# Attention units stepped between parts of the big products in a two-layer transformer half

## The reference, cut to what matters

```
for layer in range(2):                                  # first block
    h = rmsnorm(x, norm_mix[layer])
    z = h @ w_in[layer]                                 # 1024 -> 2964
    o_a = nsa_mixer(...)      # slc, win, cmp branches: 3 softmax attentions, 4 heads of 64
    o_b = diff_mixer(...)     # two softmaxes a head, one subtracted; head rmsnorm
    o_c = mlstm_mixer(...)    # conv, gates, decay-weighted attention; head rmsnorm, times sigmoid
    o_d = dilated_mixer(...)  # attention over keys at strides 1, 4, 16
    x = x + concatenate([o_a, o_b, o_c, o_d]) @ w_out[layer]
    h = rmsnorm(x, norm_ffn[layer])
    x = x + (silu(h @ w_gate[layer]) * (h @ w_up[layer])) @ w_down[layer]
x = rmsnorm(x, norm_final)
for layer in range(2):                                  # second block
    x = conformer or gated convolution, layer norm
    x = mixture of 32 experts over all tokens, layer norm
```

## Time and profile before

| | us |
|---|---|
| median of 3 runs (2234.66 to 2235.66) | 2235.55 |
| the profiled execution | 2232.91 |
| its span, first to last instruction | 2231.1 |
| TensorE busy (share of span) | 2112.0 (95%) |
| VectorE busy | 671.6 (30%) |
| ScalarE busy | 327.8 (15%) |
| GpSimd busy | 83.3 (4%) |
| mean granted TensorE clock | 0.940 |

### The profile page before, as it was taken

One profiled execution on the slowest core, in us unless ns is written; L12 is line 12 of the kernel. 1 busy time (PEld: TensorE's weight loads), 2 busy tenths in 40 slices (PEclk: granted clock), 3 DMA queues, 4 the chain that ended last, 5 costly groups with the idle time before them and its releaser, 6 DMA issues.

```text
span 2231.1 us, 23016 instructions
## 1 busy us (share of the span) xinstructions
PE 2112.0 (95%) x9082; PEld 1217.3 (55%) x9082; DVE 671.6 (30%) x1263; ACT 327.8 (15%) x777; POOL 83.3 (4%) x124
## 2 busy tenths in 40 slices
PE   8988999999988999999899999999898899999996
PEld 4566667665565767776544444443585444444442
DVE  2254333323262333256411111111423311111113
ACT  2243000011241000022210111110101111111010
POOL 3101000001002000020000000000000000000000
PEclk9866999999858999999899999999998899999999
DMA  9311777563104777644389999999824499999995
GB/s 277 87 57 10 264 256 264 196 243 108 57 1 164 263 259 269 228 145 148 150 330 421 427 427 427 428 429 426 341 113 189 196 426 427 425 427 428 427 428 225
DMA packets 154934, 603.12 MB, mean 270 GB/s; under 512 B 16688, under 2 KB 72880, under 8 KB 127440
## 3 DMA queue, kind: packets, MB, share of 16 engines
q1 hardware_dynamic: 149728, 591.43, 67.8%
q0 software_dynamic: 4752, 10.20, 1.8%
q10 hardware_dynamic: 352, 0.06, 0.0%
HBM read 597.64 MB, written 1.10 MB: 268 GB/s over the span
## 4 chain that ended last, share of the span: by engine, by line
PE 90%; DVE 4%; DMA 2%; issue 1%; ACT 1%; DVEq 1%; SPq 0%; ACTq 0%
PE ps L1657 29%; PE ps L685 14%; PE ps L497 7%; PE ps L691 7%; PE ps L1643 6%; PE ps L1627 5%; PE ps L1545 4%; PE ps L664 3%; PE ps L1510 3%; PE ps L1558 3%; DMA ring<-in_e_w_up 2%; PE ps L629 2%; PE ps L607 1%; PE ps L563 1%; PE ps L562 1%
## 5 line engine op out<-in xcount | busy, mean ns | idle before, releaser
L685 PE MATMUL ps<-hT,ring 128*128 128x256 f32 x1408 | 313.3, 384 | 1.7 <-DVE hT L260 1.7
L685 PEld LDWEIGHTS ps<-hT,ring 128*128 128x128 f32 x1408 | 276.9, 198 | 33.7 <-issue 4.0
L1657 PE MATMUL ps<-ring,qkT 128*64 128x512 f32 x1024 | 226.8, 595 | 2.9 <-ACT qkT L1829 2.9
L1657 PE MATMUL ps<-ring,hT 128*64 128x512 f32 x1024 | 226.1, 594 | 3.4 <-DMA ring<-in_e_w_gate 1.9
L1657 PE MATMUL ps<-ring,late 128*64 128x512 f32 x1024 | 226.1, 594 | 2.9 <-ACT late L1816 2.9
L497 PE MATMUL ps<-ring,hT 128*128 128x512 f32 (+1 forms) x384 | 166.1, 591 | 3.4 <-DMA ring<-in_w_in 1.9
L1657 PEld LDWEIGHTS ps<-ring,hT 128*64 128x64 f32 x1024 | 71.9, 137 | 153.4 <-issue 146.5
L1657 PEld LDWEIGHTS ps<-ring,late 128*64 128x64 f32 x1024 | 72.8, 137 | 150.7 <-issue 150.7
L691 PE MATMUL ps<-ring,late 128*128 128x512 f32 x352 | 154.7, 592 | 0.0
L1657 PEld LDWEIGHTS ps<-ring,qkT 128*64 128x64 f32 x1024 | 72.4, 137 | 136.3 <-issue 134.5
L1643 PE MATMUL ps<-qkT,O 128*128 128x256 f32 x512 | 138.7, 417 | 3.0 <-DVEq L2062 3.0
(11 more groups left out here) (367 smaller groups left out, 1818.6 us busy)
## 6 DMA issues: line engine op xcount, KB each, us to landing
ring<-in_e_w_gate SPq DMA_DIRECT2D x64, 2048.0 KB, 15.1
ring<-in_e_w_down SPq DMA_DIRECT2D x64, 2048.0 KB, 13.5
ring<-in_e_w_up SPq DMA_DIRECT2D x64, 2048.0 KB, 16.2
ring<-in_ada_w SPq DMA_DIRECT2D x24, 2048.0 KB, 9.6
ring<-in_w_gate SPq DMA_DIRECT2D x22, 1024.0 KB, 8.2
ring<-in_w_up SPq DMA_DIRECT2D x22, 1024.0 KB, 10.1
ring<-in_w_down SPq DMA_DIRECT2D x22, 1024.0 KB, 12.6
ring<-in_w_in SPq DMA_DIRECT2D x8, 2048.0 KB, 14.2
```

The source lines that it names most:

```text
L685: last = mm(m.ps[:, c, at:at + SEQ], w[:, j, c, :], m.hT[:, j, :], start=(j == 0), stop=(j == KC - 1))
L1657: last = mm(m.ps[x * T:(x + 1) * T, out + n, :], operand[:, j, at + x * T:at + (x + 1) * T], w[x][:, j, n * 512:(n + 1) * 512], start=(j = ...
```

## The change

z products can be issued in halves of four contraction steps, and w_out products in parts of two steps for one tile. The attention units now run in the middle of these. Only the chunks NSA, U, MIX and DIFF are computed ahead of the units, with scores of units 0 and 1 between them. In each unit's round TensorE issues transposed(u), one piece of dense work (`ahead_of_values`), values(u), scores(u+2), and for some u a batch (`behind_scores`). The dense piece is half a tile of z VALUES or DIL for units 0 to 7 and a part of w_out for units 9 to 13; unit 8 has four transposes.

PSUM is laid out anew: one pair of banks for scores (0, 1), one pair for transposes and values together (2, 3), z in 4 and 5, batches in 6 and 7, w_out sums in 4 to 7. Slots are too: U lies in slot 5, MIX in 1, VALUES in 3, DIL in 4; w_out is loaded to slots 5 and 2, attention buffers lie in slot 0 and half of 1. The compression batch moves behind scores(4), the order of units changes (cmp 0 ahead of dil), and the head norms are one step for mlstm and one for diff.

The core of the diff; of moved lines only the new place is shown:

```diff
-CHUNKS = ((0, ((0, 512),)), (1, ((1420, 1932),)), (5, ((512, 652), (1932, 2196))), (2, ((652, 1164),)), (3, ((2196, 2708),)),
-          (4, ((1164, 1420), (2708, 2964))))
+CHUNKS = ((0, ((0, 512),)), (5, ((1420, 1932),)), (1, ((512, 652), (1932, 2196))), (2, ((652, 1164),)),
+          (3, ((1164, 1420), (2708, 2964))), (4, ((2196, 2708),)))
-UNITS = [("slc", 0, 0), ("mlstm", 0, 0), ("slc", 1, 0), ("mlstm", 1, 0), ("diff", 0, 0), ("diff", 1, 0), ("diff", 0, 1),
-         ("diff", 1, 1), ("win", 0, 0), ("dil", 1, 0), ("dil", 0, 0), ("win", 1, 0), ("cmp", 0, 0), ("cmp", 1, 0)]
+UNITS = [("slc", 0, 0), ("slc", 1, 0), ("mlstm", 0, 0), ("mlstm", 1, 0), ("diff", 0, 0), ("diff", 1, 0), ("diff", 0, 1),
+         ("diff", 1, 1), ("win", 0, 0), ("win", 1, 0), ("cmp", 0, 0), ("dil", 0, 0), ("dil", 1, 0), ("cmp", 1, 0)]
-OUT_PAIRS = ((2, 3), (4, 5), (6, 7), (0, 1))
+OUT_BANK = (6, 3, 0, 1, 0)
+OUT_PARTS = ((4, 0, 2), (2, 0, 2), (0, 0, 1), (6, 0, 2), (0, 1, 2))
...
 def first_sync
+            if k < 2:
+                sp.wait_ge(s["pv"], nth(L, "pv", N_UNITS))
+            elif k == 2:
+                sp.wait_ge(s["y_ps"], nth(L, "y_ps", 4))
...
             elif u == 1:
-                sp.wait_ge(s["pv"], nth(L, "pv", len(UNITS)))
+                sp.wait_ge(s["y_ps"], nth(L, "y_ps", 4))
...
 def first_tensor
+        def z_part(n, i, part):
+            c = CHUNKS[n][0]
+            if part == 0:
+                if i == 0:
+                    pe.wait_ge(m.ring_full[c], chunk_full(L, n))
+                if n > 0:
+                    pe.wait_ge(s["z_act"] if i == 0 else s["z_dve"], nth(L, "z_act", n))
+            w = m.slot[c][:, 0:KC * chunk_width(n)].rearrange("p (j n) -> p j n", j=KC)
+            for j in range(KC // 2 * part, KC // 2 * (part + 1)):
+                last = mm(m.ps[:, 4 + i, 0:chunk_width(n)], m.hT[:, j, i * P:(i + 1) * P], w[:, j, :], start=(j == 0), stop=(j == KC - 1))
...
+        def out_part(i, first):
+            for c in range(2):
+                w = m.w_out[c].rearrange("p (j n) -> p j n", j=KC)
+                for j in (first, first + 1):
+                    last = mm(m.ps[:, 4 + 2 * i + c, :], m.hT[:, j, i * P:(i + 1) * P], w[:, j, :], start=(j == 4), stop=(j == (7, 1)[i]))
...
+        def ahead_of_values(u):
+            if u < 4:
+                z_part(C_VALUES, u // 2, u % 2)
+            elif u < 8:
+                z_part(C_DIL, u // 2 - 2, u % 2)
+            elif u == 8:
+                pe.wait_ge(s["o_final"], nth(L, "o_final", 1))
+                out_transposes(0)
+            elif u == 9:
...
+                out_ready(0)
+                out_part(0, 4)
+            elif u == 10:
+                pe.wait_ge(s["prep_ev"], nth(L, "prep_ev", N_PREP))
+                out_part(1, 4)
+            elif u == 11:
+                out_ready(1)
+                out_part(0, 2)
+            elif u == 12:
+                out_part(1, 2)
+            else:
+                out_ready(2)
+                out_part(0, 0)
+                out_transposes(3)
+        def behind_scores(u):
+            if u == 1:
+                diff_batch()
+            elif u == 2:
+                cmp_batch()
+            elif u == 8:
+                dil_batch()
+            elif u == 10:
+                pe.wait_ge(s["o_final"], nth(L, "o_final", 2))
+                out_transposes(1)
+            elif u == 12:
+                pe.wait_ge(s["masked"], nth(L, "masked", N_UNITS))
+                out_transposes(2)
+        for u in range(N_UNITS):
+            transposed(u)
+            ahead_of_values(u)
+            values(u)
+            if u + 2 < N_UNITS:
+                scores(u + 2)
+            behind_scores(u)
+        out_ready(3)
+        out_part(0, 6)
+        out_part(1, 6)
+        pe.wait_ge(s["o_done"], nth(L, "o_done", N_UNITS))
+        out_transposes(4)
+        out_ready(4)
+        out_part(1, 0)
...
 def first_scalar
+        for u in range(N_UNITS):
+            transposed_out(u)
+            if u == 1:
+                z_out(C_VALUES)
+            if u == 5:
+                z_out(C_DIL)
+                head_root(0)
+            if u == 8:
+                out_taken(0)
+            if u == 9:
+                head_root(1)
+            if u + 2 < N_UNITS:
+                exponentials(u + 2)
...
+            if u == 8:
+                qk(B_DIL, T_DQ, 4)
+            if u == 10:
+                out_taken(1)
+            if u == 12:
+                out_taken(2)
...
 def first_vector
+        for u in range(N_UNITS):
+            if u + 1 < N_UNITS:
+                probabilities(u + 1)
+            if u == 3:
                 z_out(C_VALUES)
+            if u == 7:
+                z_out(C_DIL)
+            unit_out(u)
+            if u + 2 < N_UNITS:
+                masked(u + 2)
+            if u == 4:
+                sub_squared(0)
+            if u == 5:
+                sub_scaled(0)
+            if u == 6:
+                dve.wait_ge(s["z_act"], nth(L, "z_act", C_DIL + 1))
+                rotate_dil(0)
+            if u == 7:
+                dve.drain()
+                rotate_dil(1).then_inc(s["rope"], 1)
+            if u == 8:
+                sub_squared(1)
+            if u == 9:
+                sub_scaled(1)
```

More of the change, by code:

```diff
@@ new lines, in cmp_batch @@
+        def cmp_batch():
+            pe.wait_ge(m.ring_full[1], (L + 1) * 64)
+            pe.sem_inc(m.seen, 1)
+            pe.wait_ge(s["blocks"], nth(L, "blocks", 1))
+            dst = batch(B_CMP)
+            cw = m.cmp_w
+            for l in range(CMP_LEN):
+                mm(dst[0:HD, 0:N_CMP], cw[0:HD, l, :], m.blocks[0:HD, l, :], start=(l == 0), stop=(l == CMP_LEN - 1))
+                last = mm(dst[0:N_CMP, 512:512 + HD], m.blocks[HD:P, l, :], cw[HD:P, l, :], start=(l == 0), stop=(l == CMP_LEN - 1))
+            last.then_inc(s["prep_ps"], 1)
@@ L742, in qk, with exponentials @@
         def qk(b, at, count):
[L743 removed]
+            src = banks(m, 6, 2)[:, 0:count * SEQ].rearrange("p (s t) -> p s t", t=SEQ)
             evac(b, m.qkT[:, at:at + count, :], src).then_inc(s["prep_ev"], 1)
+        def exponentials(u):
+            kind, t, g = UNITS[u]
+            nk = keys_of(kind, t)
+            act.wait_ge(s["masked"], nth(L, "masked", u + 1))
+            if u >= 2:
+                act.wait_ge(s["pt_ps"], nth(L, "pt_ps", u - 1))
+            scale = 1.0 if kind == "mlstm" else 32 ** -0.5 if kind == "diff" else HD ** -0.5
+            for v in range(4):
+                h = VIEW[v]
+                bias = m.nM[:, t, h:h + 1] if kind == "mlstm" else m.nmx[u % 2][:, v:v + 1]
+                a(m.pr[:, u % 2, v, 0:nk], m.sm[:, u % 2, v, 0:nk], ACT.Exp, bias=bias, scale=scale, accum_out=m.zs[u % 2][:, h:h + 1])
+            act.drain().then_inc(s["exps"], 1)
@@ L897, in first_vector, with masked @@
         last.then_inc(s["blocks"], 1)
-        z_out(C_DIFF)
+        z_out(C_MIX)
+        dve.wait_ge(s["z_act"], nth(L, "z_act", C_MIX + 1))
+        dve.drain()
+        for i in range(TILES):
+            rotate(v, dve, m, m.rz_x, m.tmp_dve, i, [(z_heads(m, i, Z_KW, 1, HD), 0, 1, HD)])
+        v.tensor_copy(m.rz_x[:, :, HD:2 * HD], m.rz_x[:, :, 0:HD]).then_inc(s["rope"], 1)
+        def masked(u):
+            kind, t, g = UNITS[u]
+            nk = keys_of(kind, t)
+            b = u % 2
+            dve.wait_ge(s["scores"], nth(L, "scores", u + 1))
+            if u >= 2:
+                dve.wait_ge(s["exps"], nth(L, "exps", u - 1))
+            mask = {"cmp": m.cmp_mask, "dil": m.dil_mask}.get(kind, m.causal)[:, t, 0:nk]
+            sm = m.sm[:, b, :, 0:nk]
+            src = m.rb[:, :, 0:nk] if kind == "mlstm" else scores_of(m, u)
+            if kind == "mlstm":
+                dve.drain()
+            last = tt(sm, src, bcast(mask.unsqueeze(1), [P, 4, nk]), ALU.add)
+            if kind != "mlstm":
+                dve.drain()
+                v.reduce_max(m.mx[b], sm, axis=AX)
+                dve.drain()
+                last = ts(m.nmx[b], m.mx[b], -(32 ** -0.5 if kind == "diff" else HD ** -0.5), None, ALU.mult)
+            last.then_inc(s["masked"], 1)
+        masked(0)
         g = m.grow
-        gates = banks(m, prep_bank(B_WIN), 2)[0:NH, 512:1024]
+        gates = banks(m, 6, 2)[0:NH, 512:1024]
         dve.wait_ge(s["prep_ps"], nth(L, "prep_ps", B_WIN + 1))
@@ L1181, in ring_counts @@
 def ring_counts():
-    loads = [DEPTH * per for per in (2, 2, 1, 1, 2, 4)]
-    frees = [6 if c in (0, 1, 5) else 2 for c in range(N_SLOTS)]
+    loads = [DEPTH * per for per in (1, 4, 2, 2, 1, 2)]
+    frees = [DEPTH] * N_SLOTS
     out = {}
```

601 lines of the change are left out of this document (267 added, 334 removed).

## The result

The changed kernel takes 2196.38 us in the median of four runs (2194.55 to 2197.45), the kernel before beside it 2235.11: a ratio of 0.9828, interval 0.9813 to 0.9842. The forecast was 2198, faster. The profiled execution took 2197.37 us against 2232.91 before, 35.5 less, at a mean granted clock of 0.959 against 0.940.

The account below looks back on a forecast made before the run. TensorE's half-clock small matmuls, short waits and clock recovery bound the attention stages. Per layer 225.3 - 204.8 - 1.6 = 18.9 us saved, 38 for both: profiled 2232.9 to 2195, median 2198 (2190 to 2212, chance 0.50).

Parts of the forecast that it names:

- Part 1: Order up to the first unit: z 52.9, batches 7.2, two scores 1.7, 1.5 allowed for ScalarE; T(0) starts at 63.3 us.
- the batch: Compression batch behind scores(4): moved, not changed, 18.0 us as before, mostly at half clock.
- hole 1: Unit 8: only four transposes to put in, TensorE waits about 5 us, clock lost; round 10 takes 12.3 instead of 7.7.
- hole 2: Unit 11: out_part(0, 2) waits for ScalarE's out_taken(1), clock down again; round takes 13.5 us instead of 8.35.
- The bound: Attention stages: small matmuls at half clock, short waits on VectorE and clock recovery cost time; the stretch averaged 225.3 us.
- The pieces: Full-clock prices: scores 1.05 us (256 keys), values 0.95 (eight instructions), transposes 0.45 (four); exponentials 2.45, copy 1.02, 0.6 or 0.4.
- The ring: Units 4 to 13: scores, mask, exponentials, copy and values set each round, dense half product inside; first round 7.4 us.
- (a): Rival: clock lost only in the compression batch, units 8 and 11 keep it; 26.9 us a layer, 2182; chance 0.20.
- (b): Rival: clock lost in nearly every unit, seven more times, only dense parts paying 1.8 each; 2223 us; chance 0.15.
- (c): Slower rival: clock lost likewise, small matmuls at half too, 3.4 us a unit; 2246; chance 0.10 for both slower rivals together.
- (d): Slower rival: ScalarE's order puts dense parts after the waits everywhere; 2268 us; chance 0.10 for both slower rivals together.
- Part 4: Outside the units: head norms counted in the rounds, tail plus 1.6 us on 4.96, SyncE's queue nothing, at worst 2 a layer.

Follow-up runs that it names:

- kernel without stepping: Changed kernel with z computed ahead of unit 0 and five w_out parts behind the last unit; new layout kept: 2283.22 us, ratio 1.0215.
- five blocks: Changed kernel with the compression batch cut into five parts, behind scores(4) to scores(8): 2180.81 us, ratio 0.9754.
- woven kernel: Against the kernel with the compression batch in five parts: its steps put two by two between the products of A(3) to A(6): 2175.32 us.
- thinned: Changed kernel with six of eight steps of VALUES and DIL tiles and half of five w_out parts left out: 2185.38 us, ratio 0.9775.
- changed tail: Changed kernel with tile 0's norm and its transposes ahead of the last w_out part for tile 1: 2201.3 us, ratio 0.9853.
- early copy: Changed kernel with ScalarE copying transposed(u+1) ahead of exponentials(u+2) in every round: 2187.64 us, ratio 0.9789.

## Why the prediction was right, step by step

| step | forecast | layer 0 | layer 1 |
|---|---|---|---|
| Part 1: first z product to T(0) | 63.3 | 64.1 | 62.0 |
| to scores(5), with the batch | 111.5 | 113.2 | 112.8 |
| of this the batch | 18.0 | 19.7 | 19.0 |
| rounds from scores(5) | 7.4, 6.35, 7.3, 6.4, 8.0 | 7.30, 6.09, 7.24, 7.17, 8.76 | 7.30, 6.10, 7.23, 6.38, 8.76 |
| round of unit 10, behind hole 1 | 12.3 | 9.74 | 9.85 |
| next | 6.0 | 6.22 | 6.21 |
| round behind hole 2 | 13.5 | 14.07 | 14.13 |
| scores(13) to the end | 24.2 | 24.3 | 24.3 |
| z to last w_out product | 204.8 (203.0 + 1.8) | 204.2 | 203.1 |
| tail | 4.96 + 1.6 | 6.6 | 6.6 |

**The bound.** TensorE loses its clock in small work: right. (The first dip lies in slices 2 to 4 of the clock row, not 3 to 5 as the prediction reads it; nothing in the sum rests on that.) Of the three things that it says cost time, the short waits gave nothing on balance: what the dense parts fill, the new ring opens again, and TensorE's idle time in the stage is as long as before. The kernel without stepping is the same finding made large, with the clock at 0.50 in every window from 150 to 185 us.

**The pieces.** Estimates of S, V and T at full clock came from rows at half; from start to start they are now 1.06 (256 keys), 1.04 (eight instructions) and 0.50 (four), where 1.05, 0.95 and 0.45 were forecast. The copy and the exponentials were as said.

**The ring** (Part 3) held to 0.3 us in the first three rounds. The fourth was 0.8 longer in layer 0, as the clock fell for a part of it (granted 0.66 in 145 to 150 us, the dense part at 147.97 took 4.19), and in layer 1, where the clock held, it took the forecast time. So the 1.8 that the prediction added for one more loss is 0.8 in one layer and nothing in the other. The fifth was 0.8 longer in both, and this belongs to the hole: values(8) stands behind it in the same round and takes 1.90 from start to start, where eight instructions take 1.0 at full clock; the prediction charged the half clock only from the next round on.

**The batch** was mis-sized by 1.7 in layer 0 and 1.0 in layer 1: in layer 0 it ran at full clock for its first seven rows only, then at 0.32 for two instructions where 0.21 is the full rate. Before, it held the clock longer: 1.00 from 70 to 75 us, 0.50 only then.

**The two holes** were put at the right places with the right size (5 forecast, 4.70 and 4.64 measured) and the clock fell behind both. The term that was off is the price of the first: 12.3 forecast, 9.74 measured. The prediction let the dense part A pay for the return of the clock, 5.7; it took 3.65. The clock had come back ahead of it, behind 6.3 us of values, scores and transposes without a pause (0.50 in 160 to 165, 0.88 in 165 to 170). That small work had already been counted at half clock, and the dense part was then charged for the return a second time. It does not hold for every kind of small work: the batch ran for 18 us without a pause at 0.50. At unit 11 nothing small stood between the hole and the dense part, and there it took 6.5.

**The errors cancel,** in layer 0: +0.8 to T(0), +0.9 up to scores(5), +1.1 in five rounds, -2.6, +0.2, +0.6, +0.1. Together +1.1 on the 203.0, where 1.8 had been allowed. So the total is closer than its terms, which are off by up to 2.6, and that is luck. So is a part of the last step: the stages gave 40.2 us where 38 was forecast, and 4.7 of it came back outside them.

**The rules weighed.** In the batch the clock was 0.50 with TensorE busy for 5.00 of 5.00 us, and in five blocks it fell with no wait at all around them; the holes lost the clock too. The Trainium skill, "TensorE: Matmul & The Clock Gate", "Why this matters for your kernels", puts drops of the clock down to idle gaps between bursts of matmuls: at the holes the trace agrees, in the batch it does not, and the woven kernel shows that the mixture of the work decides there. That consistent bubbles can mean that PSUM ran out (the Trainium skill, "Trainium Kernel Development and Optimization", "Best Practices") spoke against this change, and the experiments bear it out as a limit of what is left: each reordering that took one wait away met the next one of the shared pair of banks, 2.35 us ahead of transposes in one kernel, 2.11 to 2.87 in another.

**The rivals.** (a) did not come, the clock fell behind both holes. Its 196.8 also does not come out of the terms that the prediction prints: 12.3 against 7.7, 13.5 against 8.35 and the 1.8 make 11.6 less than 204.8, not 8.0, unless the second hole keeps a part of its price at full clock, which is not said. (b) and (c) are what happens in the thinned and unstepped kernels, so the mechanism is real; it came with parts of a quarter or half the size, or with none. (d): values waited for ScalarE's copy, as said, behind the dense part and not ahead of it, except at unit 11.

**Part 4.** The tail was right (6.6 against 6.56). The queue of SyncE cost nothing that shows: the FFN of layer 0 to the first z product of layer 1 is 247.6 us against 246.9, and that product waits 0.81 for VectorE as before.

**Open.** The waits ahead of values(4) and values(6) are alike, 1.80 and 1.71 us. In layer 0 the clock fell behind the second alone, in layer 1 behind neither, and in layer 0 of the kernel with the changed tail, whose code is the same up to there, behind both; why is not settled. The same holds for T(0), where it fell behind a wait of 0.99 us in layer 1 and not in layer 0. What of the 4.7 us outside the stage is the change and what is the scatter of the second block isn't either.

## What to carry to other kernels

Put dense matmuls inside the waits of a chain of small ones, in pieces large enough to hold the clock (half a tile of 3.6 us did, a quarter of it did not): here the pieces cost little, 60 us of them for 11 us of time, and the small work got cheaper. Then compare TensorE's idle time as well as the total: here it stayed the same, and the whole gain was clock. Small matmuls in a block lose the clock without any idle time, the same ones woven between dense products keep it, at 0.7 us more for each dense part. Before moving a step ahead, write the ring down bank by bank: here each wait that was removed showed the next one on the same banks, and the early copy paid more on top of the batch in parts, and from unit 8 on only (12.9 us), than alone and everywhere (8.7).

## What the runs showed that I had not expected

- The clock depends on the order of the same instructions with TensorE busy all the time: 1.00 woven into dense products, down to 0.50 at times in five blocks, 0.50 but for its first 1.5 us in one block.
- Leaving out 60 us of dense work saved 11 us, and made single rounds longer (8.70 us against 7.30).
- The clock returns during small work as well: behind the hole at unit 8 it was back after eight instructions of values, eight of scores and sixteen of transposes, 6.3 us in all, before any dense product (0.88 in 165 to 170 us).
